# A chunked RWKV-7 recurrence whose independent chains run in common beats, with its token space on the other half of the partitions

## The reference, cut to what matters

```python
def wkv7(r, w, k, v, a, b):                     # all (B, T, H, N) float32, H = 16, N = 64, T = 512
    def step(S, inp):                           # S: (B, H, N_v, N_k), zero at the start
        r_t, w_t, k_t, v_t, a_t, b_t = inp
        sa = jnp.einsum('bhvk,bhk->bhv', S, a_t)
        S = S * w_t[:, :, None, :] + sa[..., None] * b_t[:, :, None, :] + v_t[..., None] * k_t[:, :, None, :]
        return S, jnp.einsum('bhvk,bhk->bhv', S, r_t)
    ...
# then: y is normalised per head, and the bonus sum(r * k * r_k) * v is added
```

## Time and profile before

| | us |
|---|---|
| median of the runs | 2024.97 |
| profiled execution | 2027.18 |
| its span, first to last instruction | 2025.4 |
| the stage: L2182's first matmul to L2347's first | 214.46 to 428.00 |

### The profile page before, as it was taken

The page is one execution under the profiler, slowest core; times in us unless marked ns, Lnnn a source line. Parts: engine busy times, 40 slices in busy tenths (PEclk is TensorE's granted clock), DMA queues, the critical chain, the costliest instruction groups (busy, mean ns, idle before and its releaser), DMA issues.

```text
span 2025.4 us, 35146 instructions
## 1 busy us (share of the span) xinstructions
PE 1967.9 (97%) x14308; PEld 1602.1 (79%) x14308; DVE 1158.7 (57%) x1805; ACT 783.1 (39%) x1399; POOL 207.3 (10%) x164
## 2 busy tenths in 40 slices
PE   7999999999999999998999999999999999999997
PEld 3877899877787887775777887877888888888885
DVE  6789666576434444466475747485555256556423
ACT  7767333334222222437532222134243244344211
POOL 2000222200202012004202102020000010000001
PEclk9999999999999999998999999999999989999999
DMA  5320000222333222220244454534531222332421
GB/s 194 138 94 22 3 4 4 86 102 82 102 101 94 93 94 84 90 89 32 91 161 159 153 171 141 191 141 144 171 104 32 65 92 83 106 101 83 148 92 42
DMA packets 61004, 201.48 MB, mean 99 GB/s; under 512 B 8000, under 2 KB 11200, under 8 KB 59584
## 3 DMA queue, kind: packets, MB, share of 16 engines
q1 hardware_dynamic: 60096, 192.93, 28.7%
q10 hardware_dynamic: 768, 6.55, 1.0%
HBM read 190.68 MB, written 6.42 MB: 97 GB/s over the span
## 4 chain that ended last, share of the span: by engine, by line
PE 71%; issue 17%; DVE 7%; ACT 2%; POOL 2%; DMA 0%; DVEq 0%; POOLq 0%; SPq 0%; ACTq 0%
PE bank L2033 17%; PE bank L2035 17%; PE bank L2034 17%; POOL HS L2843 2%; PE bank L2218 1%; PE bank L2250 1%; PE bank L2265 1%; PE bank L2222 1%; DVE GBZ L1435 1%; DVE HR L1618 1%; PE bank L2519 1%; DVE wlo L1251 1%; PE bank L2505 1%; PE bank L2539 1%; PE bank L2682 1%
## 5 line engine op out<-in xcount | busy, mean ns | idle before, releaser
L1251 DVE TENSOR_TENSOR wlo<-raw,whi 128x1024 fp32r<-128x1024 f32 x270 | 327.3, 1222 | 568.9 <-ACT whi L696 566.3
L696 ACT ACTIVATE whi<-raw 128x1024 fp32r<-128x1024 f32 x270 | 282.3, 1057 | 708.6 <-PE bank L2035 695.7
L2033 PE MATMUL bank<-inh,whi 128*128 128x512 f32 x1200 | 470.7, 392 | 1.9 <-DVE inl L1495 1.6
L2035 PE MATMUL bank<-inh,wlo 128*128 128x512 f32 x1200 | 467.1, 389 | 0.0
L2034 PE MATMUL bank<-inl,whi 128*128 128x512 f32 x1200 | 467.0, 389 | 0.0
L2033 PEld LDWEIGHTS bank<-inh,whi 128*128 128x128 f32 x1200 | 225.2, 188 | 58.3 <-issue 6.6
L2035 PEld LDWEIGHTS bank<-inh,wlo 128*128 128x128 f32 x1200 | 225.2, 188 | 47.1
L2034 PEld LDWEIGHTS bank<-inl,whi 128*128 128x128 f32 x1200 | 225.3, 188 | 46.8 <-issue 0.7
L2033 PE MATMUL bank<-hidh,whi 128*128 128x512 f32 x576 | 228.5, 397 | 8.2 <-DVE HR L1618 5.5
L2035 PE MATMUL bank<-hidh,wlo 128*128 128x512 f32 x576 | 224.5, 390 | 0.0
L2034 PE MATMUL bank<-hidl,whi 128*128 128x512 f32 x576 | 224.3, 389 | 0.0
(11 more groups left out here) (423 smaller groups left out, 2853.0 us busy)
## 6 DMA issues: line engine op xcount, KB each, us to landing
raw<-in_mlp_w SPq DMA_DIRECT2D x128, 512.0 KB, 3.6
ADW<-in_w_ada SPq DMA_DIRECT2D x32, 768.0 KB, 5.0
raw<-in_w_up SPq DMA_DIRECT2D x44, 512.0 KB, 3.5
raw<-in_w_in SPq DMA_DIRECT2D x28, 512.0 KB, 3.7
raw<-in_a_w_rkv SPq DMA_DIRECT2D x24, 512.0 KB, 3.5
raw<-in_w_down SPq DMA_DIRECT2D x22, 512.0 KB, 3.5
raw<-in_a_wo SPq DMA_DIRECT2D x8, 512.0 KB, 7.6
raw<-in_b_wq SPq DMA_DIRECT2D x8, 512.0 KB, 3.4
```

Of the source, the lines that this page charges most:

```text
L696: act.activation(whi[u % SLOTS][:, :], raw[u % SLOTS][:, :], ACT.Copy).then_inc(w_hi, 1)
L1251: dve.tensor_tensor(lo[:, :], r[:, :], h[:, :].bitcast(F32), ALU.subtract).then_inc(w_lo, 1)
L2033: pe.matmul(o, w[:, wc], xh, start=start, stop=False)
L2035: return pe.matmul(o, r[:, wc], xh, start=False, stop=stop)
```

## The change

Four things change; the arithmetic is the same but for the decay, which moves from the state to its readers.

1. **Token space on the other half.** For head h, the score products and W are written to `cross(h) = head(1 - h)`: they read the partitions of one half and write those of the other, in the two array tiles off the diagonal. Masks, triangular matrices, `VT` and the inverse then live on the other half, and work within the token space lies on the diagonal again.
2. **Common beats.** There are 50 beats. Each has three sections on PE: A (left product of one level of one chunk, alternating with `off`, which is the next state and the output of a step, or with a copied score job), B (`values_sum`, `output_states` and `solved` of the neighbouring steps, alternating in some beats with a copied score job) and C (the right product of the level that began a beat earlier, alternating with a masked or copied score job). `correction` follows C. One inverse step starts per beat, with x alternating (ten beats to a group of two chunks), and the recurrence takes two tiles `cb` per step, so that eight steps fit in a group's ten beats. The recurrence of a group runs one group behind its inverse.
3. **Banks.** Left and right product of chunk x share `PB[x]`; masked scores alternate between `PB[2]` and `PB[7]`; copied scores use `PB[3]`; W is in `PB[4]`, U, the state's part of the output and the values' part of W lie in `PB[5]` and are taken by one ACT copy (`DIAG`), the next state and output are in `PB[6]`. The bonus goes through `PB[4]` to `PB[6]`, one call at the end of each of the first eight beats. Six score jobs run ahead of the first beat.
4. **Other engines.** DVE adds `PB[4]` and the copied part into `WB`, adds the two parts of the output, and adds states with the decay in one instruction per tile (`TS` is gone). POOL multiplies the decay into `AT` and `RT` of each chunk but the first. ACT no longer copies outputs one tile at a time; it squares them once per chunk.

The tables of the beats, and SP's wait:

```diff
+        PER, RPER = 2 * LEVELS, CB
+        BEATS = PER * GROUPS + RPER + 2
+        MASKED = {0: (0, 3), 1: (0, 4), 2: (2, 0), 4: (2, 1), 5: (1, 3), 7: (1, 4), 8: (3, 0), 9: (3, 1)}
+        COPIED = {0: (0, 5), 1: (2, 2), 3: (0, 6), 4: (0, 7), 6: (1, 5), 7: (3, 2), 8: (1, 6), 9: (1, 7)}
+        AHEAD_OF_TIME = (((0, 0), 2), ((0, 1), 4), ((0, 2), 3), ((1, 0), 6), ((1, 1), 7), ((1, 2), 5))
+        def inverse_at(beat):
+            return (beat // PER, beat % PER // 2, beat % 2) if 0 <= beat < PER * GROUPS else None
+        def recurrence_at(beat):
+            g, i = beat // PER - 1, beat % PER
+            return g * RPER + i if 0 <= g < GROUPS and i < RPER else None
...
-            sp.wait_ge(STEP["pe_rec"].sem, STEP["pe_rec"].at(("y", NCH // 2 - 2, 2 * CB - 1)))
+            sp.wait_ge(STEP["pe_rec"].sem, STEP["pe_rec"].at(("off", RPER * (GROUPS - 1) - 1)))
```

ACT and then DVE, one beat after the other:

```diff
+            for beat in range(BEATS + 1):
+                q, u, c, r = inverse_at(beat), recurrence_at(beat - 1), job_at(COPIED, beat), recurrence_at(beat - 3)
+                w2 = recurrence_at(beat + 1)
+                if q:
+                    act.wait_ge(pi.sem, pi.at(("q", *q)))
+                    act.activation(QS[q[2]][:], pairs(PB[q[2]][:]), ACT.Copy).then_inc(ai.sem, ai.step(("q", *q)))
+                if u is not None or w2 is not None:
+                    part = slice(2 * P if u is None else 0, 2 * P if w2 is None else 3 * P)
+                    act.wait_ge(pr.sem, pr.at(("diag", beat)))
+                    act.activation(DIAG[beat % 2][:, part], PB[5][:, part], ACT.Copy).then_inc(ar.sem, ar.step(("diag", beat)))
+                if c:
+                    score_copy(*c, 3)
...
+            for beat in range(BEATS):
+                z, m, w, y = inverse_at(beat - 1), job_at(MASKED, beat), recurrence_at(beat), recurrence_at(beat - 2)
+                if y is not None:
+                    if y < RPER * GROUPS - RPER // 2:
+                        states_next(y)
+                    outputs(y)
+                if z:
+                    inverse_sum(*z)
+                if m:
+                    score_mask(*m, masked_bank(beat))
+                if w is not None:
+                    corrections(w)
+                if beat == 0:
+                    turned(0, 0, 1)
+                if z:
+                    g, lv, x = z
+                    if lv < LEVELS - 1:
+                        turned(g, lv + 1, x)
...
+            def corrections(r):
+                dve.wait_ge(pr.sem, pr.at(("w", r)))
+                dve.wait_ge(STEP["act_rec"].sem, STEP["act_rec"].at(("diag", beat_of(r) - 1)))
+                dve.tensor_tensor(WB[r % 2][:], PB[4][:, 0:P], W2[(beat_of(r) - 1) % 2], ALU.add).then_inc(dr.sem, dr.step(("w", r)))
```

PE: where a score product lies, the waits ahead of sections A and B, the correction, and the beat itself:

```diff
+            def score_wide(j, job, bank, a):
+                cb = a + 4 * (job % 3)
+                for h in range(2):
+                    hs = head(h)
+                    mm = pe.matmul(PB[bank][cross(h), chunk(a)], (BT if job < 2 else KT)[hs, cb, tok(j)], RA[hs, :, cb, tok(j)], start=True, stop=True)
...
+            def inverse_left_ready(g, lv, x):
+                pe.wait_ge(psc.sem, psc.at(("lm", 2 * g + x, lv)))
+                if lv > 0:
+                    pe.wait_ge(din.sem, din.at(("z", g, lv - 1, x)))
...
+            def off_ready(r):
+                pe.wait_ge(arc.sem, arc.at(("diag", beat_of(r) + 1)))
+                if r > 0:
+                    pe.wait_ge(drc.sem, drc.at(("y", r - 1)))
...
+            def solved(r, n):
+                j, cbs = chunk_of(r)
+                cb = cbs.start + n
+                if n == 0:
+                    pe.wait_ge(drc.sem, drc.at(("w", r)))
...
+                for n in range(2):
+                    cb = cbs.start + n
+                    for h in range(2):
+                        mm = pe.matmul(PB[4][cross(h), tok(n)], AT[head(h), cb, tok(j)], SM[j % 2][head(h), cb, :], start=True, stop=True)
...
+                if y is not None:
+                    off_ready(y)
+                if q:
+                    inverse_left_ready(*q)
+                for n in range(CB):
+                    if q:
+                        inverse_left(*q, n)
+                    if y is not None:
+                        off(y, n)
+                    elif c and c_at == 0:
+                        score_narrow(*c, 3, n)
+                if c and c_at == 1:
+                    score_free(COPIED, beat)
+                if w2 == 0:
+                    pe.wait_ge(dp.sem, dp.at(("bonus", CB - 1)))
+                elif u is not None or w2 is not None:
+                    pe.wait_ge(arc.sem, arc.at(("diag", beat - 1)))
+                for n in range(CB):
+                    if n in (0, 1) and w2 is not None:
+                        mm = values_sum(w2, n)
+                        if n == 1 and u is None:
+                            mm.then_inc(pr.sem, pr.step(("diag", beat)))
+                    if n in (2, 3) and u is not None:
+                        output_states(u, n - 2)
+                    if n in (4, 6) and u is not None:
+                        mm = solved(u, n // 2 - 2)
+                        if n == 6:
+                            mm.then_inc(pr.sem, pr.step(("diag", beat)))
+                    if c and c_at == 1:
+                        score_narrow(*c, 3, n)
+                if z:
+                    pe.wait_ge(ain.sem, ain.at(("q", *z)))
+                    pe.wait_ge(din.sem, din.at(("t", *z)))
+                if m:
+                    score_free(MASKED, beat)
+                if c and c_at == 2:
+                    score_free(COPIED, beat)
+                for n in range(CB):
+                    if z:
+                        inverse_right(*z, n)
+                    if m and n % 2 == 0:
+                        score_wide(*m, masked_bank(beat), n // 2)
+                    if c and c_at == 2:
+                        score_narrow(*c, 3, n)
+                if w is not None:
+                    correction(w)
+                if beat < CB:
+                    bonus(beat)
+                if beat == VSUM_AT:
+                    early_sums()
```

POOL's new work:

```diff
+            def scaled(j):
+                if j > 0:
+                    pool.wait_ge(STEP["dve_score"].sem, STEP["dve_score"].at((j, 4)))
+                    for ap in (AT, RT):
+                        pool.tensor_tensor(ap[:, :, tok(j)], ap[:, :, tok(j)], FS[:, :, j - 1:j].to_broadcast([P, CB, HC]), ALU.mult).then_inc(
+                            pc.sem, pc.step(("scaled", j)))
```

More of the change, by code:

```diff
@@ L347, in program @@
         SM = [at(f"SM{x}", 80 + 2 * x, [CB, HD]) for x in range(2)]
[L348 to L350 removed]
+        WB = [at(f"WB{n}", 200 + 0.5 * n, [P]) for n in range(2)]
+        DIAG = [at(f"DIAG{n}", 201 + 1.5 * n, [3 * P]) for n in range(2)]
+        UB, Y3, W2 = ([d[:, n * P:(n + 1) * P] for d in DIAG] for n in range(3))
         FS = at("FS", 6.5, [CB, NCH])
@@ L846, in _ @@
             ai, at_, ar, ag = (STEP["act_" + n] for n in ("inv", "tok", "rec", "gn"))
[L848 to L862, removed]
@@ new lines, in _ @@
+            act.activation(small[:, 94:95], small[:, 0:1], ACT.Sqrt).then_inc(ar.sem, ar.step("table"))
+            for (j, job), bank in AHEAD_OF_TIME:
+                if job == 2:
+                    score_copy(j, job, bank)
+            for beat in range(BEATS + 1):
[10 more added lines that the diff above has]
+                    score_copy(*c, 3)
+                if r is not None and r % (RPER // 2) == RPER // 2 - 1:
+                    j = chunk_of(r)[0]
+                    act.wait_ge(dr.sem, dr.at(("y", r)))
+                    act.activation(KT[:, :, tok(j)], RT[:, :, tok(j)], ACT.Square).then_inc(ar.sem, ar.step(("y", j)))
+                if beat == VROOT_AT:
+                    act.wait_ge(STEP["pe_gn"].sem, STEP["pe_gn"].at("early"))
+                    act.activation(KNI[:, 0:EARLY], PB[0][:, 0:EARLY], ACT.Sqrt, scale=1.0 / HD, bias=small[:, 1:2]).then_inc(ag.sem, ag.step("early root"))
@@ L2336, in _, with bonus @@
-            for g in range(NCH // 2 + 1):
-                for j in (2 * g, 2 * g + 1):
-                    if j < NCH:
-                        scores(j)
-                if g > 0:
-                    recurrence(g - 1)
-                if g < NCH // 2:
-                    inverse(g)
+            psc = STEP["pool_score"]
+            def bonus(cb):
+                if cb == 1:
+                    pe.wait_ge(atk.sem, atk.at((1, 2)))
+                elif cb < 3:
+                    pe.wait_ge(dsc.sem, dsc.at(((0, 1), None, (1, 0))[cb]))
+                else:
+                    pe.wait_ge(dp.sem, dp.at(("bonus", cb - 3)))
+                pe.matmul(PB[4 + cb % 3][:], spread_of(selt, cb), RKS[rows_of(cb), :], start=True, stop=True).then_inc(pp.sem, pp.step(("bonus", cb)))
@@ new lines, in early_sums @@
+            def early_sums():
+                pe.wait_ge(arc.sem, arc.at(("y", NCH - 3)))
```

(7 more changed lines are left out.)

417 lines of the change are left out of this document (187 added, 230 removed).

## The result

The changed kernel takes 2015.5 us (median of five, 2013.6 to 2016.6) against 2026.5 for the kernel before in the same session: a ratio of 0.9936, 95% interval 0.9922 to 0.9949. I had forecast 1980. The stage, from the first score matmul to the variance matmuls behind it, takes 201.8 us in the profiled execution against 213.5, and I had worked out 167.4. So 11.7 of the 46.1 us came.

What follows compares the result with a forecast made beforehand. PE's own pace was the bound, two of four tiles working. Score jobs 5.5, first group 29.6, groups 2 to 4 110.4, end 21.9: stage 167.4 against 213.5 us, hence 1980; likeliest range 1968 to 2000, to 2022 with clock and cap.

Steps and rivals of the forecast that it cites:

- The chance at four tiles: Stage's matmuls: four 64 by 64 tiles work at once, 58 ns per record and tile; chance 0.70.
- Two at a time: Rival, beat sections: off-diagonal tile pair runs only after the diagonal one; stage 242 us, time 2054, slower; chance 0.11.
- Its number for the whole, 2020: Estimate by the skill's rule of about 25 ns between matmul starts: stage 208 us, time 2020, no change.
- The wait: Before section A, PE waits for DVE's sum after section C: 1.07 us from last start to first, about 0.8 idle.
- DVE, ACT, POOL: Other engines keep up: DVE 3.2 us a beat with mask, ACT 1.8 at most, POOL 20.3 of 36.8 a group.
- Section A ... 16 x 58.4 ns = 0.93 us: Each beat's left product: 32 records on two tiles take 0.93 us; work beside it on the other pair costs nothing.
- a group of ten 29.3 + 7.45 = 36.8 us: Ten beats of 2.93 us (wait 1.07, A 0.93, C 0.93) plus section B's 7.45; three such groups make 110.4.
- A cap on the rate of records: Rival, whole stage: PE perhaps fed no faster than 24 ns per record; +36 us, 2015; chance 0.10.
- The clock: Rival, stage: PE's idle waits lower the granted clock; eight 7 us stretches give 2000, throughout 2084; chances 0.07 and 0.02.

Runs made afterwards that it cites:

- the halved runs: Changed kernel, calls halved in number and doubled in columns: inverse products only, 1982.9 us; all narrow calls, 1971.5; all, with kinds apart within sections, 1978.7.
- the run with all calls halved: Changed kernel with all the stage's narrow calls halved in number, doubled in columns, odd blocks' own weights left out: 1971.5 us, ratio 0.9716.
- the many small calls: Changed kernel plus 12 extra calls of 64 columns ahead of each correction of beats 10 to 37 (24 beats): 2027.5 us, ratio 0.9989.

## Why the prediction was wrong

**The chance at four tiles: right.** I took 14.6 ns per record from bursts of other shapes; 63 records in 0.94 us are 15. The rival *Two at a time* (starts over 26 ns apart in section A) is out. The rule of the Trainium skill (TensorE: Matmul & The Clock Gate, "Wait — 56ns, not 53.3ns?") that matmul starts are never closer than about 25 ns does not hold between different tiles in this trace: there they come 15 ns apart on the mean for 0.9 us, and many of them 6 to 7 ns apart. Its number for the whole, 2020, was near, for another reason.

**The wait: right.** 1.07 us from the last start of C to the first of A forecast, 1.09 to 1.27 measured where PE waited only for the sum; 27 such waits in beats 10 to 38, 0.77 us idle each (0.8 forecast).

**DVE, ACT, POOL: right.** The outputs and corrections of 128 columns took 0.28 us (0.33 taken); POOL's product is late three times in the halved runs, by 1.0 us at most. `G2` never held PE: its load starts at 390.4 us, and no wait in the end of the stage names it. (My additions have small slips: DVE's beat adds up to 3.3 us and not 3.2, and the chances of slower and no change to 0.13 and 0.05 and not 0.12 and 0.06. Nothing hangs on them.)

**The step that failed** is "Section A ... 16 x 58.4 ns = 0.93 us" as the price of a section in every beat, and with it "a group of ten 29.3 + 7.45 = 36.8 us". It holds for as long as PE has its instructions. I counted columns and never instructions: a beat with both jobs has 352, and 3.7 us for it asks 95 per us. The measured feed is 64 to 67 over the 138 to 150 us of these beats, 256 in 3.86 to 3.99 us, so the group took 47 to 48 us instead of 36.8. The mechanism of my sum is what the run with all calls halved shows: beats of 3.51 us, stage 156.5. With the full number of calls the feed alone asks, as an estimate, 12,400 PE instructions / 67 = 185 us for the stage. The end, with 1280 in 27 us, is below that rate on the mean, but it has three of the gaps too.

**The rival I priced but misplaced.** *A cap on the rate of records* had chance 0.10: "perhaps PE is not fed faster", 24 ns per record, 2015, which is the time that came; only by this rival and the clock's did my range reach up to it, so that it holds the result is luck. Its mechanism was nearly this one, its size was not: I read the cap off a burst of 15 records, and it is no distance between starts at all. Inside a portion of 256 the starts are 15 ns apart; over several portions 30 to 32. The trace of before held a hint: two tiles at full pace take 2 / 29.2 ns = 68 instructions per us, its densest 20 us have 68 and the whole stage 59, and nowhere did it show more for longer than some portions. That it also had four gaps of 0.5 to 1.7 us at the 256th instruction I had passed over as noise by the load of `G2`.

**The clock.** 0.98 over beats 10 to 38, 1.00 with all calls halved. The 0.98 are two stretches of 3.4 us at the lower level, from 332.9 and 370.4 us. At half the pace they cost at most 1.7 us of array time each, so 3.4 of the 30.8 us that these beats were late; the rival *The clock* happened, but small.

What stays open: why the next packet starts 0.9 us after PE enters a portion at one time and 2.9 us at another (its move then takes 0.9 to 1.4 us, and 1.3 to 1.6 us pass until PE uses it), whether the feed is as slow where no trace is recorded (each time here comes with one), and why the halved calls shortened the end by 7 us, of which I can name the gaps (4.6 us on "issue" in the end of the kernel after) but not the rest.

## What to carry to other kernels

Count a dense stretch in instructions as well as in columns. In the starved stretches of this case PE got 64 to 67 instructions per us over 138 to 150 us (matmul, weight load and semaphore together; an fp32 call of one tile is four). By that, as an estimate, calls that the array could take faster than one in about 60 ns are bound by the feed and not by the array. Sharing the array among four tiles pays where calls are long, and where they are short only for as long as the instructions in store last, here at most the rest of one portion and the next; there merge calls, widen them, or give them to an engine with time to spare, and watch that engine next. Read "issue" gaps by their distance in instructions: multiples of 256, each ending 1.3 to 1.6 us after a packet of the instruction queue has landed, are the signature.

## What the hardware showed unexpectedly

PE's instructions come in packets of 16,384 bytes, 256 at a time; in beats 10 to 38 packets start 3.3 to 5.5 us apart, 3.86 on the mean where demand was highest (the many small calls). In this stage no trace shows a portion used sooner than 1.2 us after its packet has landed. Four 64 by 64 fp32 tiles work at once, 15 ns per record of 64 columns. A record for a busy tile does not hold those behind it for other tiles, up to six records. Bare semaphore instructions on PE come 110 ns apart (41 in 4.4 us). Transposing 32 partitions by 256 fp32 elements on DVE takes 436 ns, against 700 for 128 by 512.
